# Copying the score masks of the dilated heads into PSUM with VectorE, and adding the products to them

## The reference

```python
DIL_CONFIGS = ((128, 1), (512, 4), (2048, 16))      # window, dilation; side = window // (2 * dilation) = 64
def dilated_group(q, k, v, dilation, side):
    ...
    valid = (c >= a)[None] & (c <= a + 2 * side)[None] & (key_pos >= 0) & (key_pos < L)
    s = jnp.einsum('brhnqd,brhnkd->brhnqk', qb, kb).astype(jnp.float32) * (D ** -0.5)
    s = jnp.where(valid, s, NEG_INF)
    m = jnp.max(s, axis=-1, keepdims=True)
    p = jnp.exp(s - m)
    den = jnp.sum(p, axis=-1)
    o = jnp.einsum('brhnqk,brhnkd->brhnqd', p.astype(v.dtype), vb).astype(jnp.float32) / den[..., None]
```

## Time and profile before

| | |
|---|---|
| median of three runs | 3124.39 us |
| the profiled execution | 3125.37 us |
| span in its profile | 3123.6 us |
| instructions | 39088 |
| granted TensorE clock, mean | 0.985 of full speed |
| dilated heads, slots of the first to slots of the last | 2255 to 2755 us of the span |

### The profile page before, as it was taken

One profiled execution on the slowest core, in us unless ns is written; L12 is line 12 of the kernel. 1 busy time (PEld: TensorE's weight loads), 2 busy tenths in 40 slices (PEclk: granted clock), 3 DMA queues, 4 the chain that ended last, 5 costly groups with the idle time before them and its releaser, 6 DMA issues.

```text
span 3123.6 us, 39088 instructions
## 1 busy us (share of the span) xinstructions
PE 3000.0 (96%) x14522; PEld 2396.0 (77%) x14522; DVE 1280.4 (41%) x1641; ACT 939.0 (30%) x1546; POOL 1123.1 (36%) x885
## 2 busy tenths in 40 slices
PE   7999998999999999999999999999999999999998
PEld 6788776788877888888887766668788888778876
DVE  2573656211331000002435578860456665651132
ACT  3232555300121000001123356651454444530011
POOL 2424110344445444444445710003433343444443
PEclk8999999999999999999999999999999999999999
DMA  3111000211322111112113310012422323241132
GB/s 125 41 53 48 18 31 14 95 47 47 107 68 84 47 47 47 47 47 101 47 47 114 92 34 14 18 36 74 118 61 79 87 71 82 64 162 46 46 107 84
DMA packets 102914, 202.91 MB, mean 65 GB/s; under 512 B 14608, under 2 KB 27664, under 8 KB 102288
## 3 DMA queue, kind: packets, MB, share of 16 engines
q1 hardware_dynamic: 64512, 119.57, 13.5%
q10 hardware_dynamic: 38288, 81.73, 7.8%
HBM read 157.22 MB, written 31.46 MB: 60 GB/s over the span
## 4 chain that ended last, share of the span: by engine, by line
PE 79%; DVE 10%; ACT 5%; issue 2%; POOL 2%; DMA 1%; ACTq 0%; POOLq 0%; SPq 0%; DVEq 0%
PE ps L347 32%; PE ps L363 13%; PE ps L308 11%; PE ps L1843 8%; PE ps L1048 2%; PE ps L1079 1%; PE ps L2047 1%; DMA raw<-in_stream_dram 1%; DVE mla_ptl L1012 1%; ACT ps L988 1%; POOL wl L3040 1%; DVE mla_nm L1021 1%; PE ps L1064 1%; PE ps L1706 1%; PE ps L1066 1%
## 5 line engine op out<-in xcount | busy, mean ns | idle before, releaser
L3038 POOL TENSOR_TENSOR wh<-raw,zeros 128x512 fp32r<-128x512 f32 x440 | 483.0, 1098 | 1944.0 <-PE ps L347 619.9
L3040 POOL TENSOR_TENSOR wl<-raw,wh 128x512 fp32r<-128x512 f32 x440 | 639.9, 1454 | 34.5
L347 PE MATMUL ps<-hth,wh 128*128 128x512 f32 x1168 | 462.1, 396 | 0.4 <-issue 0.3
L347 PE MATMUL ps<-hth,wl 128*128 128x512 f32 x1168 | 461.8, 395 | 0.0
L347 PE MATMUL ps<-htl,wh 128*128 128x512 f32 x1168 | 461.6, 395 | 0.0
L363 PE MATMUL ps<-hth,wh 128*128 128x512 f32 x704 | 286.4, 407 | 2.1 <-DVE fox_vl L1261 2.1
L363 PE MATMUL ps<-hth,wl 128*128 128x512 f32 x704 | 280.4, 398 | 0.0
L363 PE MATMUL ps<-htl,wh 128*128 128x512 f32 x704 | 279.8, 398 | 0.0
L347 PEld LDWEIGHTS ps<-hth,wh 128*128 128x128 f32 x1168 | 219.2, 188 | 55.1 <-DVE dil_ot L2737 0.7
L347 PEld LDWEIGHTS ps<-htl,wh 128*128 128x128 f32 x1168 | 219.2, 188 | 53.7
L347 PEld LDWEIGHTS ps<-hth,wl 128*128 128x128 f32 x1168 | 219.2, 188 | 53.6
(11 more groups left out here) (427 smaller groups left out, 5637.6 us busy)
## 6 DMA issues: line engine op xcount, KB each, us to landing
raw<-in_stream_dram SPq DMA_DIRECT2D x440, 256.0 KB, 2.6
dil_stg<-dil_stg ACTq DMA_DIRECT2D x96, 128.0 KB, 2.4
dil_sz<-vd_dram ACTq DMA_DIRECT2D x12, 512.0 KB, 4.2
norm_x<-in_x_dram ACTq DMA_DIRECT2D x8, 512.0 KB, 9.0
heads_raw<-heads_dram ACTq DMA_DIRECT2D x8, 512.0 KB, 7.0
norm_x<-in_x_dram ACTq DMA_DIRECT2D x1, 4096.0 KB, 15.5
x_dram<-norm_x ACTq DMA_DIRECT2D x8, 512.0 KB, 3.1
down_x<-x_dram ACTq DMA_DIRECT2D x1, 4096.0 KB, 12.6
```

What stands on the lines that cost most here:

```text
L347: ins = nc.tensor.matmul(ps[:, bank + half, :], w[:, j % 2, c:c + P], a[:, k, HALF * half:HALF * half + HALF], start=first and q == 0, sto ...
L3038: nc.gpsimd.tensor_tensor(wh[:, s, :], raw[:, s, :], zeros[:].to_broadcast([P, HALF]), ALU.add).then_inc(w_hi, 1)
L3040: nc.gpsimd.tensor_tensor(wl[:, s, :], raw[:, s, :], wh[:, s, :], ALU.subtract).then_inc(w_split, 1)
```

## The change

For the slots with a mask (0 to 7 of each head, without slot 2 of the last head, whose bank is used by other work there) VectorE copies the mask into the bank before the scores, a new step `sd` ("seed"). The first matmul of the slot then adds to what lies in the bank instead of beginning a new sum, and the mask product goes. For the first three slots the seeds stand ahead of the loop on VectorE; the seed of slot n+3 stands directly behind `lo` of slot n, ahead of the other work there, and waits for this `lo` to be complete. TensorE's `scores` waits for the seed where it waited for `lo`. The products with the mask in the computation of the maxima stay.

```diff
+            def seeded(self, s, n):
+                return n < self.SLOTS and self.slots[n].mask is not None and (s, n) != (7, 2)
...
+                def seed(s, n):
+                    if not self.seeded(s, n):
+                        return
+                    if n < 2:
+                        a.wait(dve, f"sz{s}")
+                    elif n == 2:
+                        if s < 7:
+                            a.wait(dve, f"x{s + 1}.0")
+                    else:
+                        v.wait(dve, f"lo{s}.{n - 3}")
+                    bank = ps[:, self.RING[n % 3], :]
+                    if self.slots[n].mask == "ma":
+                        ins = nc.vector.tensor_copy(bank.rearrange("p (a b) -> p a b", a=2), self.ma[:].bitcast(F32).unsqueeze(1).to_broadcast([P, 2, 256]))
+                    else:
+                        ins = nc.vector.tensor_copy(bank, self.m1[:].bitcast(F32))
+                    v.did(ins, f"sd{s}.{n}")
+
+                dve.wait_ge(self.masks, 5)
                 first(0, 0)
                 prepare(0)
                 for s in range(self.HEADS):
+                    for n in range(3):
+                        seed(s, n)
                     for n in range(self.SLOTS):
...
                         v.did(tt(self.PTl[...], ps[...], self.PTh[...], ALU.subtract), f"lo{s}.{n}")
+                        seed(s, n + 3)
...
                 def scores(s, n):
-                    if n >= 3:
+                    seeded = self.seeded(s, n)
+                    if seeded:
+                        v.wait(pe, f"sd{s}.{n}")
+                    elif n >= 3:
                         v.wait(pe, f"lo{s}.{n - 3}")
...
-                        nc.tensor.matmul(out, self.keys(self.F, g, tile), ..., start=tile == sl.tiles[0][0], ...)
+                        nc.tensor.matmul(out, self.keys(self.F, g, tile), ..., start=not seeded and tile == sl.tiles[0][0], ...)
...
-                    if sl.mask == "ma":
+                    if sl.mask == "ma" and not seeded:
...
-                    elif sl.mask == "m1":
-                        ins = nc.tensor.matmul(ps[:, bank, :], identr[:], self.m1[:], start=False, stop=True, skip_group_check=True)
```

More of the change, by code:

```diff
@@ L2425, in between, with seeds @@
                     return flat({2: f"r2{s}", 3: f"kl{s}.2", 6: thirds(s, 2, "vl"), 7: [f"t1{s + 1}.0"] if s < 7 else []}.get(n, []))
+                def seeds(s, ns):
+                    return [f"sd{s}.{n}" for n in ns if self.seeded(s, n)]
                 def gated(s):
@@ L2436, in __init__ @@
                     "t10.0", prep_v(0),
-                    *[flat(*[flat(f"lo{s}.{n}", between(s, n)) for n in N], f"cmb{s}",
+                    *[flat(seeds(s, range(3)), *[flat(f"lo{s}.{n}", seeds(s, [n + 3]), between(s, n)) for n in N], f"cmb{s}",
                            prep_v(s + 1) if s < 7 else ["rc7", "on7"]) for s in H]))
@@ L2893, in scores @@
                         out = ps[:, bank, self.columns(g, tile, at)]
-                        nc.tensor.matmul(out, self.keys(self.F, g, tile), self.queries(self.G, g, tile), start=tile == sl.tiles[0][0], stop=False, skip_group_check=True)
+                        nc.tensor.matmul(out, self.keys(self.F, g, tile), self.queries(self.G, g, tile), start=not seeded and tile == sl.tiles[0][0], stop=False, skip_group_check=True)
                         ins = nc.tensor.matmul(out, self.keys(self.C, g, tile, R), self.queries(self.E, g, tile, R), start=False, stop=True, skip_group_check=True)
-                    if sl.mask == "ma":
+                    if sl.mask == "ma" and not seeded:
                         for tile, at in sl.tiles:
```

## The result

The changed kernel takes 3140.69 us (median of 5 runs, 3137.08 to 3144.78) against 3124.39 us (5 runs, 3122.26 to 3126.91): a ratio of 1.0054, 95% interval 1.0043 to 1.0064. It is slower by 16.3 us. Forecast were 8.7 us and a range that ended at 3139.5: right in the sign, too small by nearly half. Its profiled execution has a span of 3143.0 us against 3123.6. It is the slowest of the five (3144.78 us), so the profile shows somewhat more loss than the median has.

What follows compares the result with a forecast made beforehand. The prediction took VectorE's queue, with four seeds ahead of `lo` 4, to bound the loops up to slot 4. Head delays of 3 x 1.33 + 2 x 0.90 + 0.63 + 0.64 + 1.66 = 8.7 on 3124.4 gave 3133.1 us; range 3125.5 to 3139.5.

Steps and rivals of the forecast that it cites:

- What bounds the loop: Slot loops of the dilated heads: VectorE, 41% busy over the span, becomes the bound up to slot 4; backlog 1.62 us.
- Price of a seed: VectorE's mask copy into PSUM: 0.69 us taken, between a lowest bound of some 0.42 and a highest of 0.743.
- Price of its wait: On VectorE a seed waits for `lo`: 0.04 us after its end, 0.73 from start to start.
- rival (2): Waiting for VectorE's own step is free, seeds start 0.60 behind `lo`: 3129.5 us; chance 0.09 with what lies between.
- The chain to `lo` 4: VectorE in head 2: with four seeds ahead, `lo` 4 starts 7.41 us behind `lo` 0.
- The loop at full clock: Head 2, `lo` 0 to the last values' end: 15.48 us against 14.15 before.
- The sum, 8.7: Delays of the heads' loops, from 0.63 to 1.66 us each, added up to 8.7 us later.
- the sentence on the clock: TensorE's new idle stretches of up to 1.5 us in the loops cost no clock: term of nothing.
- The cover of seed 2: Seed 2 delays the scores of slot 2 to 2395.9, still ahead of the values at 2396.22: no cost.
- (1) cheap seeds: VectorE's seeds take 0.42 us each: 1.7 us in all, 3126.1 us; chance 0.08.
- (3) TensorE as the bound: VectorE keeps up, masks of slots 3 to 7 save 9.4 us: 3115.0; chance 0.08, smaller gains included.
- (4), seeds of 0.75 us: VectorE's seeds without overlap, 0.7 us more per head: 3138.6 us; chance 0.75 together with the forecast.

Runs made afterwards that it cites:

- e2_filler: Changed kernel plus unread products into free bank 1, two ahead of the values of slot 3 and four ahead of slot 4, heads 0 to 6: 3133.2 us.
- e1_both: Changed kernel with its seeds kept but overwritten by the first product, and the mask products made again: 3135.2 us.
- e12_after: The changed kernel measured once more, nothing altered: 3135.9 us.
- e7_first3: Changed kernel with seeds for slots 0 to 2 only, the mask products of slots 3 to 7 back: 3129.1 us.
- e8_no_seed6: Changed kernel without the seed of slot 6, whose mask product is back: 3126.9 us.
- e9_best: e5_all with `kl` behind seeds 0 and 1 instead of ahead of them: 3119.4 us.
- e3_early: Changed kernel with `kl` moved ahead of the loop behind `ql` and `r2` moved behind seeds 0 and 1: 3120.6 us.
- e5_all: e3_early with `t1` of the next head moved behind `lo` 9 and slot 2 with its mask product instead of a seed: 3118.5 us.

## Why the forecast was right in sign and wrong in size

- **What bounds the loop**: right. VectorE is 42% busy over the span and still the bound up to slot 4.
- **Price of a seed**, 0.69 us from a `lo` and an operation that writes PSUM: measured 0.687 and 0.695. The copy from SBUF to SBUF, the low bound, was the wrong neighbour. **Price of its wait**: starts 0.66 to 0.72 behind `lo`; rival (2), that waiting is free, fell. The row behind the 0.04 us was misread, though: in the program `kl` waits for a step of ScalarE and not for `lo` 3, so it shows no wait for one's own step. That the figure held for the seeds was luck.
- **The chain to `lo` 4**: 7.41 forecast, 7.39 measured. **The loop at full clock**: 15.48 forecast, 15.43 or 15.44 on even heads (e2_filler), 15.7 on odd ones, where the late DMA issues add 0.2. The sum, 8.7, against 8.1: heads 5 and 6, whose slow DMA issues I had taken as given, have none there; head 1 has one now.
- **The step that failed** is the sentence on the clock: waits of up to 1.5 us stand in the loops before, "so I count no loss of clock for them". The term stood at nothing. It measured 9.6 us in the profile, more than the queue; in the medians it is some 8 us, and some 4 in the repeat (estimates, above). The wait of 1.48 us that I took as a neighbour stands by itself ahead of the values of slot 0 of head 7. In the changed loop a wait of 1.0, one of 0.6 and one of 1.2 us come within 9 us, with fewer products between them. Each was in my own working; I priced them as time waited and not as idleness of TensorE. That the mask products also kept TensorE busy was nowhere in the sum. With seeds and mask products both (e1_both) the same three waits were 0.53, under 0.3 and 0.99 us in head 2, and the clock stayed at 1.00.
- **The cover of seed 2**: I checked that the values of slot 0 weren't late and not who else waits for the scores of slot 2. ScalarE does, with four DMA issues queued behind it: 0.5 us up to slot 3, hidden on even heads by the queue, 0.2 us on odd ones.
- **Rivals**: (1) cheap seeds and (3) TensorE as the bound fell; (4), seeds of 0.75 us, gave nearly the measured time, but for a reason that isn't there. The range ended just past it, at 3139.5, and so missed by 1.2 us. The repeat of the changed kernel, 3135.9 us, lies inside the range: how far the time was off hung in part on how often the clock fell.

## What to carry to other kernels

Work moved from a full engine to one that is idle on average has a price in the other's queue: count what stands ahead of the one step that the full engine waits for, and move the unhurried work out of that place first, for that may be the whole gain. Where TensorE gets waits in place of products, price them twice, as time and as a risk to its clock, and look at who else waits for each step that is delayed, DMA issues in a queue among them. Where a small gain is at stake, measure the stretch in the profile beside the whole time, and run the control that has the tidying without the idea.

## What the runs showed of the hardware

- The granted clock fell to 0.52, nearly the lower level, directly behind three waits of 0.99, 0.61 and 1.23 us (they end at 2402.60, 2408.05 and 2410.75 in head 2), while the products between them ran at 1.00. In one execution (e12_after) even heads with these waits ran at 1.00 twice and at 0.91 twice. The Trainium skill (TensorE: Matmul & The Clock Gate, "The HAM clock gate (the "warmup" mystery)") tells of a clock that is halved after idleness, in windows that run free of the kernel; the spread among equal loops agrees with that, though no run here shows the windows.
- Neither the number of waits nor the length of the longest decides alone. One wait of 1.77 us ahead of slot 0 of head 7 brought the clock down in e7_first3 and e2_filler (0.64 and 0.66 in the 3.4 us behind it); in e7_first3 the wait before it, 0.74 us, had ended 3.9 us earlier. In e8_no_seed6 and e9_best it passed at 1.00, as did one of 2.12 us in e3_early and e5_all.
- Six idle products of 512 columns in those waits went with full clock in seven loops of seven, in the one profile of that kernel: 3133.2 us against 3140.7 and 3135.9.
- An issue of a DMA by ScalarE took 0.5 to 0.6 us as a rule, and in single loops up to 1.9 us (2604.65 in head 5 before; its effect is in the earlier trace rows). These slow issues come in other heads in other kernels; their cause wasn't looked for.
